# All 16,384 experts computed densely in place of gathered rows, in a two-block transformer kernel

## The chip, the core and the metric

The kernel runs on one core of a Trainium2 chip. A core has a matrix engine (TensorE, "PE" in the profile; its weight loads are "PEld"), a vector engine (VectorE, "DVE"), a scalar engine (ScalarE, "ACT"), GpSimd ("POOL", used here almost only to issue transfers), and SyncE ("SP", which issues the weight transfers). Sixteen DMA engines move data between DRAM and the on-chip memory SBUF; matrix products land in PSUM, eight banks of 128 x 512 floats. All data are 32-bit floats. The metric is the device time of one execution in microseconds (us), the median of three runs.

## The reference, cut to what matters

For 256 tokens of width 1024 a first block (attention with a chosen set of keys, a convolution branch, a mixture of experts called PEER, and a gated per-layer projection) is followed by a second block (a recurrent scan over a context and over the tokens, then a convolutional feed-forward). The change is in the experts and in the first part of the context's scan. Per token and for each of 8 heads, PEER forms two queries, scores each against 128 keys, takes the best 16 of either side, then the best 16 of the 256 pairs, which name 16 experts out of 128 x 128:

```python
def peer(h, w_query, sub_keys, expert_u, expert_v):
    q = (h @ w_query).reshape(B, S, PEER_HEADS, 2, PEER_HALF)
    sc = jnp.einsum('bshcd,hckd->bshck', q, sub_keys)
    sv, si = lax.top_k(sc, PEER_TOPK)
    ...
    cand_i = (si[..., 0, :, None] * N_KEYS + si[..., 1, None, :]).reshape(B, S, PEER_HEADS, n_cand)
    top_s, top_j = lax.top_k(cand_s, PEER_TOPK)
    eidx = jnp.take_along_axis(cand_i, top_j, axis=-1)
    gate = jax.nn.softmax(top_s.astype(jnp.float32), axis=-1).astype(h.dtype)
    ...
        u = expert_u[et]
        v = expert_v[et]
        act = jax.nn.gelu(jnp.einsum('tnd,td->tn', u, xt)) * gt
        return jnp.einsum('tn,tnd->td', act, v)
```

So 128 experts per token: a dot product with a row u of 1024, gelu, a gate, and a sum of rows v of 1024. Both tables hold 16,384 rows, 67.1 MB each.

## The kernel before, in words

One program per engine is written out by hand; engines meet only by semaphores. A list called order (from L2582) holds stages: all engines do a stage's functions one after the other. Dense products use two ring slots of weights (2 MB each, loaded by SP, L479 to L484: tile i waits until tile i-2 is used) and two halves of PSUM, G[0] and G[1]. The helper for a tile whose weights stand still (stationary) while 256 tokens stream is L502, the one with tokens stationary and 512 weight columns streaming is L512.

The stages are: projections and attention (L741 to L873), the mix (to 275 us of the trace), pe_queries (L1234 on: norm, first query tiles, first scores at L1260), then a stage called beside, then the gated projection (pe_ple, L741 and L752), the token scan (pe_x_in and the pairs), and the feed-forward (L502, L2454).

In the stage beside, POOL gathers for each of 256 steps (two blocks of 128 tokens, 128 selections each) one row of 8 KB for each of 128 partitions: u and v of one expert (L1475). Eight such row buffers are in flight. VectorE forms the dot product of a row's u half with the token (L1490), ScalarE applies gelu and the gate and builds a small diagonal (L1496, L1501, L1506), TensorE multiplies the diagonal with the v half and adds into PSUM (L1521), which frees the buffer. A list of pieces says what every engine does between two such groups: the other query tiles (L1269), the choice of experts by VectorE (dve_select, L1364 on), then the context: normed, transposed (L2147), projected (L2157), and the context's scan (L1741, L1751, L1808, L1822, L1942 and L1984 to L1988 in pe_pair, L2105). The context's weights and the last token block arrive by SP behind sp_ctx.

Of the kernel before, what the change touches and what calls it, by code (L numbers as in the profile page):

```python
# [19 lines left out]
F32 = mybir.dt.float32  # L20
# [36 lines left out]
RING = 8  # L57
GROUP = 2
QUADS, QP = 4, 32
# [21 lines left out]
def const_columns():  # L81


    widths = dict(ident=P, eps=1, gn_eps=1, flip=P, lower=CH, upper=CH, lower_eq=CH, upper_eq=CH, lower_neg=CH, upper_neg=CH, head_mean=P, head_mean2=2, conv_mean=P,
                  ident2=HD, hide=TB * T, reset=RC * T, iota=NCAND, ident_q=QP, quad=QUADS)
    at, out = 0, {}
    for name, n in widths.items():
        out[name] = (at, n)
        at += n
    return out, at  # L90


def consts_array():
# [27 lines left out]
    put("iota", np.arange(NCAND, dtype=np.float32)[None])  # L121
    put("ident_q", np.eye(QP)[i % QP])
    put("quad", (i[:, None] // QP) == np.arange(QUADS)[None])
# [18 lines left out]
def weight_tiles(dram):  # L142
# [28 lines left out]
    tile("ctx_k", part(w, 0, DC, K20, 512))  # L171
    tile("ctx_v", part(w, 0, DC, V20, 512))
    tile("ctx_lora", part(w, 0, DC, LORA0, 128), width=128)
    for i in range(2):
        tile(f"ple_proj{i}", part(dram["w_ple_proj"], 0, 2, 512 * i, 512))
# [16 lines left out]
def build(nc, dram, out_dram):  # L192
# [5 lines left out]
    with ExitStack() as ctx:  # L198
# [112 lines left out]
        r = Region()  # L311
        eidx = r.take(TB * NSEL, U32).rearrange("p (b n) -> p b n", b=TB)
        gate = r.take(TB * NSEL).rearrange("p (b n) -> p b n", b=TB)
        dots, gelu, acts = [r.take(RING).rearrange("p (g n) -> p g n", n=GROUP) for _ in range(3)]
        diag = r.take(RING * QP).rearrange("p (g n) -> p g n", g=RING)
        rows = r.take(RING * 2 * D).rearrange("p (g n) -> p g n", g=RING)
        high = r.take(2 * D).rearrange("p (g n) -> p g n", g=2)
        quad_ring = ring[:, tile_at["ple_proj0"] % WSLOTS, 1024:4096].rearrange("p (g n) -> p g n", g=QUADS - 1)
        after_rows = r.at

        carry = r.take(512)
        loraup = r.take(2 * 512).rearrange("p (d n) -> p d n", d=2)
        after_mod = r.at
        gatebc = Region(after_mod).take(2 * D).rearrange("p (g n) -> p g n", g=2)
        hold = after_mod + 2 * D

        qpT = chunks(16)
        qpT_end = r.at
        rest = r
        r = Region(ARENA - 3072)  # L330
        keysT = r.take(2 * PH * NK).rearrange("p (g n) -> p g n", g=2 * PH)
        gbc = r.take(D)
        r = rest
# [8 lines left out]
        tsc = r.take(HEADS * PK).rearrange("p (g n) -> p g n", g=HEADS)  # L342
# [3 lines left out]
        eif = r.take(HEADS * PK)  # L346
        gsum = r.take(HEADS)
        spread_e, spread_g = [r.take(HEADS * PK * QUADS) for _ in range(2)]
        assert r.at <= ARENA - 3072
        sel_end = r.at  # L350
# [3 lines left out]
        r = Region(after_mod)  # L354
        a2 = actT.rearrange("p c t -> p (c t)")
# [4 lines left out]
        def scan_memory(full, r, free, beside=None):  # L360
# [13 lines left out]
            m.b, m.kd = tile(), tile(free[0])  # L374
            m.cum, m.e = tile(), tile(free[1])
# [13 lines left out]
            if full:  # L389
# [5 lines left out]
        ctx_m = scan_memory(False, r, [a2[:, 0:1024], a2[:, 1024:2048]],  # L395
                            ring[:, tile_at["ctx_lora"] % WSLOTS, 1024:4096])
        ctx_end = r.at
# [8 lines left out]
        x_m = scan_memory(True, r, [r.take(1024), r.take(1024)])  # L406
# [13 lines left out]
        quad_last = Region(ctx_end).take(D)  # L420
        pT = normed[:, 0, 0:512].rearrange("p (k t) -> p k t", k=2)
        pproj = high
        sgate = Region(after_rows - 4096).take(2048).rearrange("p (b n) -> p b n", b=TB)
# [23 lines left out]

        ctok = Region(after_mod + 1024).take(TB * D).rearrange("p (b n) -> p b n", b=TB)
        cnormed = keysT.rearrange("p g n -> p (g n)").rearrange("p (b n) -> p b n", b=TB)
        assert ctx_m.lora.shape[-1] and after_mod + 3 * 1024 + T <= qpT_end  # L450
# [13 lines left out]

        def sp_weights(sp):
            for i, (name, width, parts) in enumerate(tiles):
# [4 lines left out]
                if name == "ctx_lora":  # L471
                    sp_ctx(sp)
                if name == "ple_proj1":
                    sp_last_tokens(sp)
                if name == "ple_gate0":
                    sp.wait_ge(S("cdone"), 1)
                    sp.wait_ge(S("dots_ok"), TB * GROUPS)
                if i >= WSLOTS:
                    sp.wait_ge(S("tile_done"), i - WSLOTS + 1)  # L479
                for view, kc, at, n in parts:  # L480
                    dst = ring[:, i % WSLOTS, 0:kc * width].rearrange("p (k n) -> p k n", n=width)
                    sp.dma_start(dst[:, :, at:at + n], view).then_inc(S(f"landed{i % WSLOTS}"), 16)
# [3 lines left out]
        def pe_tile(pe, name, buffer=True):  # L486
# [7 lines left out]
            return ring[:, i % WSLOTS, 0:kc * width].rearrange("p (k n) -> p k n", n=width), G[i % 2]  # L494
# [48 lines left out]
        ACT_LOADS = ("lora", "ctx", "pT", "gup", "fg")  # L543
# [9 lines left out]

        NORM_ORDER = ("nc",)

        def so_far(tag, per_norm, n):

            return NORM_ORDER.index(tag) * per_norm + n

        def act_norm(act, tag, src, dst, col, ready=(), gain=False):

            for b in range(1):
                for name, v in ready:
                    act.wait_ge(S(name), v)
                nc.scalar.activation(dst[:, b, :], src[:, b, :], ACT.Square,
                                     accum_out=stat[:, col + b:col + b + 1]).then_inc(S("norm_squares"), 1)
            act.wait_ge(S("norm_squares"), so_far(tag, TB, TB))
            nc.scalar.activation(stat[:, col + 2:col + 4], stat[:, col:col + 2], ACT.Sqrt, scale=1.0 / D,  # L570
                                 bias=K("eps")).then_inc(S("norm_root"), 1)
            if not gain:
                act.wait_ge(S("norm_recip"), so_far(tag, 1, 1))
                nc.scalar.activation(dst[:, 0, :], src[:, 0, :], ACT.Copy,
                                     scale=stat[:, col + 4:col + 5]).then_inc(S("normed_ok"), 1)

        def dve_norm(dve, steps, tag, src, dst, col, gain=None, ready=()):
            for name, v in ready:
                dve.wait_ge(S(name), v)
            nc.vector.tensor_tensor_reduce(dst[:, 1, :], src[:, 1, :], src[:, 1, :], 1.0, 0.0, ALU.mult, ALU.add,  # L580
                                           stat[:, col + 1:col + 2]).then_inc(S("norm_squares"), 1)
            dve.wait_ge(S("norm_root"), so_far(tag, 1, 1))
            nc.vector.reciprocal(stat[:, col + 4:col + 6], stat[:, col + 2:col + 4]).then_inc(S("norm_recip"), 1)
            dve.wait_ge(S("norm_recip"), so_far(tag, 1, 1))
            for b in range(TB) if gain is not None else (1,):
                r_ = stat[:, col + 4 + b:col + 5 + b]
                if gain is None:
                    ins = nc.vector.tensor_scalar(dst[:, b, :], src[:, b, :], r_, None, ALU.mult)
                else:
                    ins = nc.vector.scalar_tensor_tensor(dst[:, b, :], src[:, b, :], r_, gain, ALU.mult, ALU.mult)  # L590
                ins.then_inc(S("normed_ok"), 1)

# [2220 lines left out]
```

## Time and profile before

| | |
|---|---|
| three runs | 1559.96 us median (1553.43 to 1562.26) |
| span of the profiled execution | 1554.9 us, 5.1 us under the median |
| TensorE busy | 1212.9 us, 78% of the span |
| VectorE busy | 926.5 us, 60% |
| ScalarE busy | 431.5 us, 28% |
| moved by DMA | 409.73 MB, 264 GB/s mean |

The page gives for the profiled execution its span, from the first to the last instruction, and no other time of its own; the three times are those of runs without a profile. Two things about counts: a matrix product of 32-bit floats that is one line in the code stands as two MATMUL records, so a tile of 32 products shows x64; and the merged durations of the chain and the timeline are those to read, since single records overlap.

### The profile page before, as it was taken

Reading aid. Unit: us, or ns where it says so; the run is one execution under the profiler, and the core shown is the slowest. Engines: PE = TensorE matmul, PEld = TensorE weight load, DVE = VectorE, ACT = ScalarE, POOL = GpSimd, SP = SyncE. Lnnn points to the kernel's source line nnn. Section 1 sums busy time; section 2 is a strip of 40 time slices with the busy share of each in tenths; the row PEclk is TensorE's granted clock in tenths of the full one; section 3 lists DMA queues with packets and bytes.
Section 4 is the critical chain, followed back from the end, with each engine's and each line's share of the span. In section 5 each row is a group of like instructions: output and inputs, shape, how many; then the busy total and the mean of one; then the engine's idle time right before and its main releaser. Section 6 shows DMA issues by size and latency. Waiting matters only on the chain.

```text
span 1554.9 us, 26679 instructions
## 1 busy us (share of the span) xinstructions
PE 1212.9 (78%) x11282; PEld 834.9 (54%) x11282; DVE 926.5 (60%) x2067; ACT 431.5 (28%) x1094; POOL 347.1 (22%) x315
## 2 busy tenths in 40 slices
PE   7989898894385533457856775799987888999998
PEld 6467784772153100125524452468877774888843
DVE  2887666657797988785677655321455343455512
ACT  2111420132432422543364332423243211110100
POOL 1000012034354555454455544000000000000000
PEclk9997999996597855569878996899999999999999
DMA  9551459699999999999999999624300023344432
GB/s 381 195 191 66 144 205 390 238 383 419 414 410 420 420 422 421 421 414 419 416 421 420 420 418 418 240 82 163 109 9 3 4 111 108 122 163 161 137 140 104
DMA packets 109720, 409.73 MB, mean 264 GB/s; under 512 B 8456, under 2 KB 33552, under 8 KB 76448
## 3 DMA queue, kind: packets, MB, share of 16 engines
q0 software_dynamic: 44576, 297.35, 46.5%
q1 hardware_dynamic: 63552, 106.48, 19.2%
q10 hardware_dynamic: 1472, 4.20, 1.0%
q8 instruction: 88, 1.44, 0.4%
q14 instruction: 32, 0.26, 0.0%
HBM read 405.89 MB, written 2.11 MB: 262 GB/s over the span
## 4 chain that ended last, share of the span: by engine, by line
PE 58%; DMA 22%; DVE 10%; ACT 4%; issue 3%; POOL 2%; another core or an unknown queue 0%; POOLq 0%; DVEq 0%; ACTq 0%; SPq 0%
PE psum L502 20%; DMA arena<-in_experts,arena 17%; PE psum L1942 8%; PE psum L2454 5%; PE psum L512 4%; DVE arena L1490 4%; PE psum L1521 3%; DMA arena<-in_lora_up 2%; PE psum L755 2%; PE psum L1269 2%; POOL arena L1475 2%; PE psum L2244 2%; PE psum L760 2%; DMA arena<-in_ada_wT 2%; PE psum L741 2%
## 5 line engine op out<-in xcount | busy, mean ns | idle before, releaser
L1475 POOL DMA_INDIRECT arena<-in_experts,arena x256 | 317.1, 1239 | 383.2 <-PE psum L1521 299.8
L1521 PE MATMUL psum<-arena 128*32 128x512 f32 x1024 | 185.4, 805 | 238.2 <-ACT arena L1506 231.6
L502 PE MATMUL psum<-actT,weights 128*128 128x256 f32 x1312 | 287.3, 381 | 0.0
L502 PEld LDWEIGHTS psum<-actT,weights 128*128 128x128 f32 x1312 | 250.3, 191 | 35.7 <-issue 1.5
L1521 PEld LDWEIGHTS psum<-arena 128*32 128x32 f32 x1024 | 22.7, 121 | 329.5 <-ACT arena L1506 307.3
L1490 DVE CUSTOM_DVE_ANT_0 arena<-arena 128x1024 f32<-128x1024 f32 x96 | 116.7, 1224 | 50.9 <-DMA arena<-in_experts,arena 50.1
L1490 DVE CUSTOM_DVE_ANT_0 arena<-weights,arena 128x1024 f32<-128x1024 f32 x96 | 116.6, 1223 | 37.1 <-DMA arena<-in_experts,arena 35.1
L1496 ACT ACTIVATE arena<-arena 128x2 f32<-128x2 f32 x128 | 26.1, 204 | 364.3 <-DVE arena L1490 350.4
L1942 PE MATMUL psum<-arena 64*64 64x64 f32 (+1 forms) x2816 | 89.7, 231 | 17.4 <-DVE arena L2059 7.1
L1942 PEld LDWEIGHTS psum<-arena 64*64 64x64 f32 x2816 | 84.1, 142 | 26.0 <-issue 14.6
L1490 DVE CUSTOM_DVE_ANT_0 arena<-normed,arena 128x1024 f32<-128x1024 f32 x64 | 77.2, 1225 | 22.1 <-DMA arena<-in_experts,arena 20.3
L1119 POOL DMA_DIRECT2D arena<-in_ada_wT x48 | 25.5, 531 | 229.7 <-DVE mod L1135 229.7
L2454 PE MATMUL psum<-weights,arena 128*128 128x512 f32 x176 | 75.7, 592 | 0.0
L512 PE MATMUL psum<-weights,actT 128*128 128x512 f32 x160 | 69.2, 592 | 0.0
L1506 ACT ACTIVATE arena<-const,arena 128x32 f32<-128x32 f32 x256 | 66.3, 306 | 0.0
L1501 ACT ACTIVATE arena<-arena 128x1 f32<-128x1 f32 x256 | 61.5, 287 | 12.1 <-ACT arena L1496 0.4
L2528 DVE SCALAR_TENSOR_TENSOR arena<-arena,small 128x256 f32<-128x256 f32 x154 | 61.9, 478 | 0.0
L2454 PEld LDWEIGHTS psum<-weights,arena 128*128 128x128 f32 x176 | 33.4, 190 | 41.7 <-issue 41.6
L1942 PEld LDWEIGHTS psum<-actT,arena 64*64 64x64 f32 x1152 | 39.3, 134 | 21.4 <-ACT arena L2027 12.0
L512 PEld LDWEIGHTS psum<-weights,actT 128*128 128x128 f32 x160 | 30.4, 190 | 37.8 <-issue 37.8
L1942 PE MATMUL psum<-actT,arena 64*64 64x64 f32 x1152 | 45.5, 221 | 5.7 <-issue 4.3
L675 ACT ACTIVATE normed<-xres 128x512 f32<-128x512 f32 (+1 forms) x13 | 9.0, 692 | 146.4 <-DVE xres L2544 60.3
(390 smaller groups left out, 1897.0 us busy)
## 6 DMA issues: line engine op xcount, KB each, us to landing
weights<-in_w_in SPq DMA_DIRECT2D x18, 2048.0 KB
arena<-in_ada_wT POOLq DMA_DIRECT2D x48, 512.0 KB, 6.3
weights<-in_ffn_w_up SPq DMA_DIRECT2D x22, 1024.0 KB
weights<-in_ffn_w_down SPq DMA_DIRECT2D x5, 2048.0 KB
weights<-in_w_out SPq DMA_DIRECT2D x4, 2048.0 KB
weights<-in_w_peer_q SPq DMA_DIRECT2D x4, 2048.0 KB
arena<-in_experts,arena POOLq DMA_INDIRECT x256
weights<-in_w_ple_gate SPq DMA_DIRECT2D x2, 2048.0 KB
```

The costliest lines, as they stand in the source:

```text
L502: mm = nc.tensor.matmul(out[:, c * T:(c + 1) * T], w[:, k, c * P:(c + 1) * P], act[:, k, :], start=(k == 0), stop=(k == kc - 1))
L512: mm = nc.tensor.matmul(out[:, b * 512:(b + 1) * 512], act[:, k, b * P:(b + 1) * P], w[:, k, :], start=(k == 0), stop=(k == kc - 1))
L741: mm = nc.tensor.matmul(chunk_bank(c)[:, b * P:(b + 1) * P], xres[:, b, c * P:(c + 1) * P], norm_diag[:, b, :], start=True, stop=True)
L755: mm = nc.tensor.matmul(out[:, 2 * i * T:(2 * i + 1) * T], w[:, k, 2 * i * P:(2 * i + 1) * P], actT[:, k, :], start=(k == 0), stop=(k == D ...
L1475: nc.gpsimd.indirect_dma_start(out=rows[:, n % RING, :], out_offset=None, in_=dram["experts"], in_offset=bass.IndirectOffsetOnAxis(ap=eidx ...
L1490: ins = nc.vector.tensor_tensor_reduce(rows[:, pos, 0:D], quad_row(b, k % QUADS), rows[:, pos, 0:D], 1.0, 0.0, ALU.mult, ALU.add, dots[:, ...
L1501: nc.scalar.activation(acts[:, g, j:j + 1], gelu[:, g, j:j + 1], ACT.Copy, scale=gate[:, b, bass.ds(t * RING + (g * GROUP + j), 1)]).then_ ...
L1506: nc.scalar.activation(diag[:, pos, :], K("ident_q"), ACT.Copy, scale=acts[:, g, j:j + 1]).then_inc(S("diag_ok"), 1)
L1521: mm = nc.tensor.matmul(SUMS[sum_part(k, i), i, :], diag[:, pos, :], rows[:, pos, D + 512 * i:D + 512 * (i + 1)], start=first, stop=last, ...
L1942: mm = nc.tensor.matmul(dst[half[c], g, at + q * n:at + (q + 1) * n], left(g, c, q), right(g, c, q), start=True, stop=True)
L2454: return nc.tensor.matmul(aux[2 * b + n], ffT[:, f, b * P:(b + 1) * P], w[:, k, 512 * n:512 * (n + 1)], start=(f == 0), stop=(f == FC - 1))
L2528: st.run(nc.vector.scalar_tensor_tensor(dst, src, w, dst, ALU.mult, ALU.add))
```

## The change

The experts are no longer gathered. Their tables are laid out as 128 chunks of u and 128 chunks of v (one chunk: the 128 experts of one first key, 512 KB), and all are computed for all tokens:

- pe_keys_of, 128 times: 8 products with a 128 x 128 piece of the u chunk stationary and 256 tokens streaming. Two chunks fill a PSUM bank; ScalarE applies gelu into SBUF (act_gelu); POOL writes each pair's result to DRAM (dots_out), but for two pairs that are kept.
- The gates become a dense matrix gsel[expert i][expert j][token]: per token one product of two one-hot matrices (pe_onehots, dve_onehots, act_onehots), 256 in all.
- pe_values_of, after all keys: per pair of chunks VectorE multiplies the results, read back by POOL, with the gates (dve_values_of), and TensorE multiplies with the v chunks: per chunk 2 token blocks x 2 halves, 512 columns streaming, all added up in four PSUM banks.
- All four query tiles and the context's norm, transposes and three projections now come in pe_queries, ahead of the first key chunk. The context's scan and the choice of experts stand between the first 64 key chunks, the one-hot products between the other 64.
- The chunks use the ring of weights in eight parts (sp_experts). The projection of p (before two ring tiles) is made at the end in pe_ple from memory of its own. The normed rows in DRAM and their copies by quarters (quads) go.

```diff
-        def pool_rows(pool):
-            for n in range(TB * NSEL):
...
-                nc.gpsimd.indirect_dma_start(
-                    out=rows[:, n % RING, :], out_offset=None, in_=dram["experts"],
...
-                ins = nc.vector.tensor_tensor_reduce(rows[:, pos, 0:D], quad_row(b, k % QUADS), rows[:, pos, 0:D], 1.0, 0.0,
-                                                     ALU.mult, ALU.add, dots[:, g, j:j + 1])
...
-                    mm = nc.tensor.matmul(SUMS[sum_part(k, i), i, :], diag[:, pos, :], rows[:, pos, D + 512 * i:D + 512 * (i + 1)],
-                                          start=first, stop=last, skip_group_check=True)
...
+        def sp_experts(sp, first, last):
+            for s in range(first, last):
+                if s >= U_SLOTS:
+                    sp.wait_ge(S("exp_used"), s - U_SLOTS + 1)
...
+        def pe_keys_of(pe, c):
+            w = pe_chunk(pe, c).rearrange("p (k n) -> p k n", k=DC)
+            pair = c // 2
+            if c % 2 == 0 and pair >= 2:
+                pe.wait_ge(S("gelu_ok"), pair - 1)
+            at = (c % 2) * T
+            for k in range(DC):
+                mm = nc.tensor.matmul(dots_bank(pair)[:, at:at + T], w[:, k, :], actT[:, k, :],
+                                      start=(k == 0), stop=(k == DC - 1))
+            mm.then_inc(S("exp_used"), 1)
...
+        def pool_dots(pool):
+            for pair in range(PAIRS - KEPT):
+                pool.wait_ge(S("gelu_ok"), pair + 1)
+                pool.dma_start(dots_out[pair], dstage[:, pair % KEPT, :]).then_inc(S(f"dots_out{pair % KEPT}"), 16)
...
+            def sums(at, c, b, w):
+                lhs = weighted[:, at % ACT_SLOTS, c * T + b * P:c * T + (b + 1) * P]
+                for n in range(2):
+                    mm = nc.tensor.matmul(aux[2 * b + n], lhs, w[:, 512 * n:512 * (n + 1)], start=(at == 0 and c == 0),
+                                          stop=(at == PAIRS - 1 and c == 1), skip_group_check=True)
+                return mm
+            for at in range(PAIRS - LAST_PAIRS):
+                w = [pe_chunk(pe, NK + 2 * at + c) for c in range(2)]
+                for b in (1, 0):
+                    pe.wait_ge(S("weighted_ok"), TB * at + 2 - b)
...
+            for g in range(T // OH):
+                pe.wait_ge(S("onehot_ok"), g + 1)
...
+                for k in range(OH):
+                    mm = nc.tensor.matmul(PS[:, g % 4, k * P:(k + 1) * P], onehots[:, g % 2, 1, k, :],
+                                          onehots[:, g % 2, 0, k, :], start=True, stop=True)
...
         def pe_ple(pe):
+            pe.wait_ge(S("ple_in"), 32)
             pe.wait_ge(S("gatebc_ok"), 2)
+            for b in range(TB):
+                for n in range(2):
+                    for k in range(2):
+                        mm = nc.tensor.matmul(G[b][:, 512 * n:512 * (n + 1)], pT[:, k, b * P:(b + 1) * P],
+                                              pw[:, k, 512 * n:512 * (n + 1)], start=(k == 0), stop=(k == 1))
+                mm.then_inc(S("pproj_pe"), 1)
+            pe.wait_ge(S("pproj_ok"), TB)
             pe_norm_tile(pe, "n3", "ple_gate0", tokens=True)
...
+        SCAN_END = 64
+        turn = 0
+        for f in scan_stages(ctx_m, "c"):
+            spread(f, turn, turn + f["pieces"])
+            turn += f["pieces"]
...
+        spread(dict(pe=pe_onehots, act=act_onehots, dve=dve_onehots, pieces=T // OH + 3), SCAN_END, NK - 2)
```

TensorE before, in the stage beside, at the first expert groups (L1521) and the last query tiles (L1269; L1260 are scores):

```order
58 L1521 MATMUL psum<-arena 32x512 x4
59 L1260 MATMUL psum<-arena 128x128 x8
60 L1269 MATMUL psum<-actT,weights 128x256 x8
61 L1521 MATMUL psum<-arena 32x512 x4
62 L1269 MATMUL psum<-actT,weights 128x256 x8
63 L1521 MATMUL psum<-arena 32x512 x4
64 L1269 MATMUL psum<-actT,weights 128x256 x8
65 L1521 MATMUL psum<-arena 32x512 x4
```

TensorE now, where the key chunks begin (L1110 is pe_keys_of; L1250 context products, L1260 scores, L514 the three context projections, the rest pieces of the context's scan):

```order
57 L1260 MATMUL psum<-arena 128x128 x8
58 L1250 MATMUL psum<-arena 128x128 x8
59 L514 MATMUL psum<-normed,weights 128x256 x72
60 L1110 MATMUL psum<-actT,weights 128x256 x8
61 L1665 MATMUL psum<-const,arena 128x2 x8
62 L2119 MATMUL psum<-const,arena 128x128 x8
63 L1110 MATMUL psum<-actT,weights 128x256 x24
64 L1675 MATMUL psum<-const,stat 64x128 x16
65 L1110 MATMUL psum<-actT,weights 128x256 x8
66 L1734 MATMUL psum<-arena 128x256 x8
67 L1110 MATMUL psum<-actT,weights 128x256 x48
```

Between two pieces there stand now 8 products of 128 x 256 where there stood 4 of 32 x 512, and the projections stand ahead of all of it.

TensorE before in the context's solves (L1942), with expert groups between the levels:

```order
134 L1521 MATMUL psum<-arena 32x512 x4
135 L1942 MATMUL psum<-actT,arena 64x64 x16
136 L1942 MATMUL psum<-arena,actT 64x64 x16
137 L1942 MATMUL psum<-actT,arena 64x64 x16
138 L1521 MATMUL psum<-arena 32x512 x4
```

TensorE now in the same solves (L1868 is the former L1942), and further on the one-hot products (L1478):

```order
72 L1868 MATMUL psum<-arena 64x64 x48
73 L1110 MATMUL psum<-actT,weights 128x256 x8
74 L1868 MATMUL psum<-arena 64x64 x48
75 L1110 MATMUL psum<-actT,weights 128x256 x8
...
420 L1478 MATMUL psum<-normed 128x128 x4
421 L1110 MATMUL psum<-actT,weights 128x256 x8
422 L1478 MATMUL psum<-normed 128x128 x4
423 L1110 MATMUL psum<-actT,weights 128x256 x8
```

The solves keep their 48 products a level; what moved is that a whole key chunk follows each, and four one-hot products come between the later chunks.

SP's transfers now, from the first query tile to the gated projection:

```order
13 L493 DMA weights<-in_w_peer_q 128x8x512
14 L561 DMA arena<-in_ctx 128x2x1024
15 L493 DMA weights<-in_w_peer_q 128x8x512 x3
16 L561 DMA arena<-in_lora_up 128x2x512
17 L493 DMA weights<-in_w_in 128x8x512
18 L493 DMA weights<-in_w_in 128x8x128
19 L1093 DMA weights<-in_expert_u 128x1024 x3
20 L493 DMA weights<-in_w_in 128x8x512
21 L1093 DMA weights<-in_expert_u 128x1024 x125
22 L1093 DMA weights<-in_expert_v 128x1024 x128
23 L493 DMA weights<-in_w_ple_gate 128x8x512 x2
```

The context's tokens are loaded behind the first query tile now, and the expert chunks stand in SP's queue between the last context tile and the gated projection's weights.

## Rows read from the trace of the kernel before

**Rows 1.** The page: the slices, chain and dearest groups.
```profile
PEclk9997999996597855569878996899999999999999
DMA  9551459699999999999999999624300023344432
...
PE 58%; DMA 22%; DVE 10%; ACT 4%; issue 3%; POOL 2%; another core or an unknown queue 0%; POOLq 0%; DVEq 0%; ACTq 0%; SPq 0%
...
L1475 POOL DMA_INDIRECT arena<-in_experts,arena x256 | 317.1, 1239 | 383.2 <-PE psum L1521 299.8
L1521 PE MATMUL psum<-arena 128*32 128x512 f32 x1024 | 185.4, 805 | 238.2 <-ACT arena L1506 231.6
L502 PE MATMUL psum<-actT,weights 128*128 128x256 f32 x1312 | 287.3, 381 | 0.0
```
**Rows 2.** Stretches: us, busy (records) of PE, PEld, DVE, ACT, POOL; PEclk, DMA, GB/s.
```profile
297.40:995.20 697.80, 429.88 (x4761) 233.14 (x4761) 512.54 (x1284) 264.44 (x816) 317.15 (x256) 0.76 1.00 409
600.00:700.00 100.00, 47.22 (x396) 15.81 (x398) 81.13 (x166) 45.29 (x128) 50.27 (x40) 0.60 1.01 418
1334.00:1473.00 139.00, 139.00 (x645) 122.17 (x644) 76.36 (x190) 17.10 (x42) 0.00 (x0) 1.00 0.44 152
```
**Rows 3.** VectorE's busy time in L1490 alone, same first stretch.
```profile
297.40:995.20 697.80, 311.29 (x512) 0.76 1.00 409
```
**Rows 4.** Chain of waits, in order of time: start, us, what.
```profile
290.43 6.92 PE psum L760 x32
298.53 2.02 PE psum L1260 x16
300.56 13.83 PE psum L502 x64
...
995.20 2.90 PE psum L741 x12
...
1334.60 138.13 PE psum L502 x640
1472.73 75.55 PE psum L2454 x176
```
**Rows 5.** Timeline of TensorE at the first expert groups.
```profile
342.49 1.07 PE L1521 MATMUL psum<-arena 128*32 128x512 f32 x8
343.49 3.72 PE L1269 MATMUL psum<-actT,weights 128*128 128x256 f32 x16
347.14 1.06 PE L1521 MATMUL psum<-arena 128*32 128x512 f32 x8
```
**Rows 6.** The token scan's solves, L1942 and L1984 alone: us, PE, PEld, PEclk, DMA, GB/s.
```profile
1142.00:1272.00 130.00, 78.32 (x2528) 74.78 (x2528) 0.97 0.07 23
...
1142.00:1272.00 130.00, 11.55 (x128) 11.00 (x128) 0.97 0.07 23
```
**Rows 7.** Chain of waits in the token scan's start.
```profile
1057.54 1.68 PE psum L1741 x16
...
1073.14 1.90 PE psum L1751 x32
...
1082.96 1.93 PE psum L1808 x16
1084.89 7.10 PE psum L2244 x32
...
1119.62 1.75 PE psum L1822 x16
1121.37 3.46 PE psum L2244 x16
```
**Rows 8.** SP's transfers of two 1 MB tiles, and a product that waited for one.
```profile
217.33 7.27 SPq L482 DMA_DIRECT2D weights<-in_w_att_out  x2
...
231.46 3.72 PE L502 MATMUL psum<-arena,weights 128*128 128x256 f32 x16 [0.35 <-DMA weights<-in_w_att_out]
```
**Rows 9.** Timeline at the end of the gathers, all engines.
```profile
984.69 0.99 ACT L1625 COPY arena<-psum 128x1024 f32<-128x1024 f32 x1
...
989.76 1.94 PE L1521 MATMUL psum<-arena 128*32 128x512 f32 x8 [3.86 <-ACT arena L1506]
...
994.76 0.29 DVE L722 TENSOR_SCALAR normed<-const,stat 128x128 f32<-128x128 f32 x1
```
**Rows 10.** Groups of VectorE, 290 to 992: busy us, mean ns, idle before.
```profile
L2059 DVE TENSOR_TENSOR actT<-actT,psum 128x512 f32<-128x512 f32 x20 | 13.7, 687 | 30.8 <-PE psum L1942 30.8
```

More of the change, by code:

```diff
@@ L170, in weight_tiles @@
     w = dram["w_in_2"]
-    tile("ctx_k", part(w, 0, DC, K20, 512))
     tile("ctx_v", part(w, 0, DC, V20, 512))
     tile("ctx_lora", part(w, 0, DC, LORA0, 128), width=128)
-    for i in range(2):
-        tile(f"ple_proj{i}", part(dram["w_ple_proj"], 0, 2, 512 * i, 512))
+    tile("ctx_k", part(w, 0, DC, K20, 512))
     for i in range(2):
@@ L463, in build, with begin_of @@
             landed_at.append(16 * n_parts[i % WSLOTS])
+        def begin_of(name):
+            return 3072 if name == "ctx_lora" else 0
         def sp_weights(sp):
@@ L577, in dve_norm @@
[L577 to L591, printed above, removed]
@@ L1227, in act_quads, with ring_chunk @@
[L1227 to L1240 removed]
+        def ring_chunk(s):
+            return ring[:, (s % U_SLOTS) // 4, 1024 * (s % 4):1024 * (s % 4 + 1)]
@@ new lines, in act_values_of, with score_bank, ctx_bank @@
+        def act_values_of(act):
+            act_gelu(act, PAIRS - 1)
+            act.wait_ge(S("weighted_ok"), TB * (KEPT + PLE_CHUNKS // 2))
+            for g in range(2):
+                act.wait_ge(S("gatebc_pe"), g + 1)
+                nc.scalar.copy(gatebc[:, g, :], G[g]).then_inc(S("gatebc_ok"), 1)
+        def score_bank(b):
+            return aux[2 + b]
+        def ctx_bank(c):
+            free = G[tile_at["ctx_v"] % 2]
+            return (aux[0], aux[1], free[:, 0:512], free[:, 512:1024])[c % 4][:, 0:T]
@@ L1526, in groups_of_rows @@
-        def groups_of_rows(eng, group, b, first, last):
-            while first < last:
-                t, g = divmod(first, PER_TURN)
-                if g or t == 0 or last - first < 2 * PER_TURN:
-                    group(eng, b, t, g, GROUP)
-                    first += 1
-                else:
-                    end = min(last // PER_TURN, TURNS - 1)
-                    if group is act_group:
-                        eng.wait_ge(S("gates_done"), TB * QUARTERS)
-                    with eng.Fori(t, end) as i:
-                        for g in range(PER_TURN):
-                            group(eng, b, i, g, GROUP)
-                    first = PER_TURN * end
@@ L2655, in build, with spread @@
-        n_groups = TB * GROUPS
-        pieces[GROUPS + 4].append((len(beside), 0))
-        beside.append(dict(act=act_ple_load, pieces=1))
-        pieces[-1].append((len(beside), 0))
-        beside.append(dict(act=act_block0_squares, pieces=1))
-        assert len(pieces) < n_groups, len(pieces)
+        FIRST = 2
+        stage(dve=lambda dve, st: dve_select_first(dve, st, FIRST))
+        beside = []
+        pieces = [[] for _ in range(NK)]
+        def spread(f, begin, end):
+            n = f["pieces"]
+            for k in range(n):
+                pieces[begin + k * (end - begin) // n].append((len(beside), k))
+            beside.append(f)
```

825 lines of the change are left out of this document (327 added, 498 removed).

## The prediction

> **What bounds the kernel now.** I read the page first: its slices show the DMA share at 9 in a block from about a fifth of the span to three fifths, with TensorE's clock at 5 to 9 of ten there and at 9 almost everywhere else; the chain of waits gives TensorE 58% and DMA 22%; the dearest groups name the gathers, L1475 [rows 1]. Then the stretch from the end of the first query tile (290.43 + 6.92 = 297.35) to the first norm product of the gated projection (995.20) [rows 4]. In these 697.8 us the DMA share is 1.00 at 409 GB/s while TensorE is busy 429.9, VectorE 512.5 and ScalarE 264.4, none of them full, and the mean clock is 0.76; one hundred microseconds inside it show 418 GB/s, clock 0.60 and TensorE 47.2 busy [rows 2]. So the transfer bounds this stretch: 256 gathers of 128 rows of 8 KB are 268.4 MB, or 642 us at 418 GB/s, and TensorE's and VectorE's work lies beneath it. Ahead of it and behind it the chain is mostly TensorE: the feed-forward runs without a gap for 139.0 us at clock 1.00 with the DMA share at 0.44 [rows 2, 4].
>
> **What one product costs.** All rests on this. L502's 640 records from 1334.60 take 138.13 us [rows 4]. In the code these are ten tiles of 32 products, so a product is two records; the whole group has 1,312 records for 20.5 tiles [rows 1], which bears that out. One product of 128 x 256 is 138.13 / 320 = 0.432 us, one of 128 x 512 is 75.55 / 88 = 0.859 us (L2454, 176 records) [rows 4], weight loads and tile changes included, at full clock (2.4 GHz, PEclk 1.00).
>
> **The change, part by part.**
>
> Gone: 268.4 MB of gathers, 311.3 us of VectorE in L1490 [rows 3], L1521 and the small ScalarE steps. As the stretch is replaced as a whole, I count what stands there now. What transfers remain are 134.2 MB of chunks and 62 results of 256 KB written and read, 32.5 MB: 399 us at 418 GB/s, far beneath what follows.
>
> Front (first query tile to first key chunk). Three more query tiles at 13.83 [rows 4] are 41.5. Four sets of scores at 2.02, and 1.2 before the first (298.53 - 297.35) [rows 4], are 9.3. Sixteen context products of 128 x 128 at 1.75 / 8 = 0.22 [rows 7] are 3.5, with about 2 for ScalarE's copies between them. The three projections are 72 products at 0.432, 31.1. The last one's weights share a ring slot with the first, so SP issues them only when that is used, with the short one (3.5) as cover. A 1 MB tile issued when a slot came free near 224.3 was waited for until 231.46 [rows 8], 7.2 us; 2 MB are at least 5.0 at 418 GB/s and at most twice 7.2, and I take 7.5, nearer the low end because no other load runs beside it: 4.0 of wait (1.5 to 11). The context's 1 MB comes earlier now, beside the modulation weights: 2.5 later for all. Sum 93.9; before, part of this lay under the transfer.
>
> Key phase. 1,024 products of 128 x 256 are 442.0. The context's scan: L1942 has 2,432 records there, at 78.32 / 2528 = 0.031 each [rows 6] 75.3; the second half of four pairs 11.6 (L1984, with its two neighbours in between) [rows 6]; two directions of four steps at 1.75 to 1.93, 15.4; the common part 1.68 + 1.90 + 1.75 [rows 7], 5.3; the chain of states, 64 products, 4: together 111.6. Before, these lay under the gathers. Between 64-wide and 128-wide products a change costs something: 8 products of L1269 beside L1521 take 3.65 (343.49 to 347.14) [rows 5] where 3.45 is the sum, and 16 of L2244 after L1808 take 7.10 where 6.91 is the sum [rows 7]. I take 0.3 for going and coming, 45 times: 13.5. The 256 one-hot products cost 0.22 each, 56.1, and 0.1 for each of 64 groups, since 16 records of L1822 and then L2244 show no more than the sum [rows 7]: 62.4. Transposes of experts and gates: 3.
>
> Waits in the key phase are the unknown cost, since no row of before shows these engines together. At least nothing: a chunk of 3.45 follows each piece, VectorE needs 0.69 for a level's sum [rows 10], and its load is half: 512.5 - 311.3 = 201 us is all else that it does in the old stretch [rows 2, 3], to which one-hots add 64 x (4 x 0.29 [rows 9] + 0.69 [rows 10]) = 118, against 1,000 us. At most about 1 us in each of the 63 turns with a piece of the scan, if the choosing of experts, which stands behind each piece on VectorE, makes the next piece wait: 63. I take 10, near the low end, as the chunk is five times the step that it hides. Sum of the key phase: 442.0 + 111.6 + 13.5 + 62.4 + 3 + 10 = 642.5.
>
> Value phase. 512 products of 128 x 512 at 0.859: 439.8. Sixteen products of 128 x 128 for the modulation's gates, 3.5; 1 at the seam, since two pairs are kept in SBUF and the next results have 13.7 us to arrive. VectorE's two products per pair are small beside 6.9 us of TensorE. Sum 444.3. If the read-back did not keep up, TensorE would wait for it; but four slots are 27 us ahead.
>
> Tail. The projection of p moved behind the last chunk: 8 products, 6.9, then a copy by ScalarE, 0.99 [rows 9], and a hop: 8.2 from the last value product to the norm's first, in place of 995.20 - (989.76 + 1.94) = 3.5 [rows 4, 9]. The norm's square sums and roots run beside it. From there on the program is the same, and its 560 us are taken over.
>
> Sum: 93.9 + 642.5 + 444.3 + 8.2 = 1,188.9 in place of 697.8, which is 491 more. The profiled execution would go from 1554.9 to 2046; the median lies 5.1 us above its span, so the forecast is **2051 us**, a ratio of 1.31.
>
> One rule would change the sum. The row says 0.859 for a 32-bit product of 512 columns [rows 4]. The Trainium skill (TensorE: Matmul & The Clock Gate, Back-to-back issue gap) gives a sustained spacing of about 131 ns per matmul at 512 columns, and N / 2.4 + 2.5 ns for a lone one; another page of the Trainium skill (FP8 and Floating Point Precision, TensorE Precision Notes) says that true 32-bit floats take four passes. By 131 ns the value phase would be an estimated 268 us, by the other formula 442. The trace agrees with the second, and a rival below carries the first.
>
> **Rivals.**
>
> Transfer still bounds. The change halves the bytes; if TensorE fitted beneath them, the stage would last 399 us, and 1560 - 697.8 + 93.9 + 399 + 8.2 = 1363: faster. For it: the DMA share of 1.00 and 409 GB/s [rows 2]. It decides from the point where a chunk's 8 products cost less than its landing, 512 KB at 418 GB/s = 1.25 us, or 0.157 a product. Against it: 0.432 in a gapless row, 2.8 times as much.
>
> A record is a product. Were 0.216 and 0.429 the full prices, both phases would lose half, 441: 1610, slower still. Against it: the count of tiles in the code.
>
> Short passes in the value phase: products of 512 columns at 0.524, so 512 x 0.335 = 171 less: 1880. Against it: 176 records at 0.429, and nothing in the value phase differs from them in shape. This is the page's first figure.
>
> The key phase waits at every turn of the scan, the high end above: 53 more, 2104. For it: VectorE and ScalarE are in line, and a solve's level waits for both. Against it: the chunk between.
>
> **How the numbers follow.** The forecast, with its small terms off by up to 40 in all (the front's wait, the changes of width, waits of 0 to 40): 0.77, 2010 to 2090. Waits at every turn: 0.16, 2090 to 2150. Short passes: 0.02; a record is a product: 0.01; transfer bounds: 0.01; still cheaper small terms, 1980 to 2010: 0.03. The range that leaves out under two in ten is 2010 to 2115. A measurement of this kernel tells 0.5% (8 us) from no change. Faster by more: 0.01; within it: 0.01, for a mixture of the cases that I have not seen; slower: 0.98.
>
> **What would show it.** In the new profile the group of L1110 should have 2,048 records and 442 us, the values' products (1,024 records) 440, both without a gap longer than a wait; PEclk 9 from the front to the end; DMA share 0.3 to 0.5 there, some 170 MB in place of 268; VectorE and ScalarE under half. The first key chunk should begin near 391, the first value product near 1034, the norm near 1486. The prediction is wrong if a product of L1110 takes clearly less than 0.43, if the clock sinks in the long run of products, or if TensorE sits idle for more than 40 us in the key phase, and then the releaser tells whether it was VectorE's choice, ScalarE's gelu or a chunk.

## The result: 2022.7 us, 1.297 times the time before

The changed kernel takes 2022.71 us (median of 4 runs, 2019.42 to 2023.77), the kernel before 1559.78 (4 runs); the ratio is 1.2971, with a 95% interval of 1.2940 to 1.3003. The forecast was 2051 in a range of 2010 to 2115. The profiled execution has a span of 2021.5 us, 24.5 below the 2046 that the sum gave for it. The section behind the experiments goes through these 24.5 us, and through the other 4 by which the median missed.

The page of the changed kernel, its slices and its chain (answering to [rows 1]):

```profile
PE   8989889899999999999999999999999978899998
...
DVE  3966655163373334444211111111123353435531
...
PEclk9979989999999999999999999999999999999999
DMA  9334874343343344444466555555324100244542
...
PE 93%; DMA 2%; DVE 2%; ACT 1%; issue 1%; DVEq 0%; POOL 0%; POOLq 0%
```

The block of 9s in the DMA row is gone and a block of 9s in the PE row has taken its place; where TensorE pauses no more, the granted clock stays at 1.00, the upper of its two levels. DMA's 22% of the chain became 2%.

The stages in windows (answering to [rows 2]; columns as there). They are the front, the key phase up to the last piece of the scan, the key phase with the one-hot products, the value phase, and all that follows:

```profile
302.42:394.46 92.04, 85.68 (x433) 76.02 (x434) 29.69 (x148) 15.28 (x24) 0.00 (x0) 0.98 0.36 126
394.46:735.90 341.44, 341.20 (x4148) 297.10 (x4148) 162.92 (x557) 94.26 (x143) 17.31 (x32) 1.00 0.39 132
735.90:1006.47 270.57, 270.57 (x1499) 244.96 (x1498) 106.72 (x312) 53.09 (x95) 16.23 (x30) 1.00 0.44 150
1006.47:1449.51 443.04, 443.04 (x1058) 198.13 (x1057) 49.10 (x127) 5.25 (x7) 35.49 (x65) 1.00 0.57 189
1449.51:2021.50 571.99, 528.61 (x5449) 409.94 (x5447) 217.65 (x409) 114.04 (x207) 0.00 (x0) 0.98 0.29 100
```

In 1,055 us of keys and values TensorE is idle for 0.24 us, while the DMA engines are half idle. Two groups of rows say where that time lies: TensorE's groups in the key phase, and the products of the value phase.

```profile
L1110 PE MATMUL psum<-actT,weights 128*128 128x256 f32 x2048 | 464.6, 381 | 0.0
L1868 PE MATMUL psum<-arena 64*64 64x64 f32 (+1 forms) x2432 | 75.5, 222 | 0.0
L1478 PE MATMUL psum<-normed 128*128 128x128 f32 x512 | 66.8, 275 | 0.0
L1910 PE MATMUL psum<-arena 64*64 64x64 f32 x128 | 11.6, 243 | 0.0
...
L1665 PE MATMUL psum<-const,arena 128*128 128x2 f32 x16 | 1.9, 250 | 0.2 <-DVE arena L1697 0.2
```

```profile
L1178 PE MATMUL psum<-weights,normed 128*128 128x512 f32 x1024 | 439.8, 592 | 0.0
```

A warning on reading the first: 464.6 us for the keys is more than they cost. A matmul's end is modelled, and the last record of each of 128 chunks overhangs the next piece by 0.17 us. The price is the distance between starts. In the timeline of TensorE (start, us, line), where a turn is one key chunk and the piece that stands beside it, a chunk of 8 products takes 3.45 us (from 850.72 to 854.17) and the 4 one-hot products of a turn 0.90:

```profile
849.83 1.05 PE L1478 MATMUL psum<-normed 128*128 128x128 f32 x8
850.72 3.62 PE L1110 MATMUL psum<-actT,weights 128*128 128x256 f32 x16
854.17 1.05 PE L1478 MATMUL psum<-normed 128*128 128x128 f32 x8
855.07 3.62 PE L1110 MATMUL psum<-actT,weights 128*128 128x256 f32 x16
```

128 x 3.45 is 442, as [rows 4] had said.

### The profile page after: what moved, and what is told of

It reads as the page before. It is cut to its first block, busy times and chain, and to the rows that moved or that the text cites. A ratio compares the mean times of both kernels' runs of the same rounds, so it can differ in the third digit from the quotient of the medians.

```text
span 2021.5 us, 31021 instructions
## 1 busy us (share of the span) xinstructions
PE 1935.2 (96%) x13670; PEld 1423.5 (70%) x13670; DVE 763.0 (38%) x1935; ACT 340.7 (17%) x559; POOL 98.2 (5%) x185
## 4 chain that ended last, share of the span: by engine, by line
PE 93%; DMA 2%; DVE 2%; ACT 1%; issue 1%; DVEq 0%; POOL 0%; POOLq 0%
PE psum L1110 22%; PE psum L1178 22%; PE psum L514 18%; PE psum L1868 8%; PE psum L2320 4%; PE psum L524 3%; PE psum L1478 3%; PE psum L688 1%; DMA arena<-in_ada_wT 1%; PE psum L2110 1%; PE psum L693 1%; PE psum L674 1%; PE psum L1910 1%; PE psum L685 1%; PE psum L806 1%
## 5 line engine op out<-in xcount | busy, mean ns | idle before, releaser
L1110 PE MATMUL psum<-actT,weights 128*128 128x256 f32 x2048 | 464.6, 381 | 0.0
L1178 PE MATMUL psum<-weights,normed 128*128 128x512 f32 x1024 | 439.8, 592 | 0.0
L1110 PEld LDWEIGHTS psum<-actT,weights 128*128 128x128 f32 x2048 | 380.5, 190 | 51.2 <-issue 1.5
L1178 PEld LDWEIGHTS psum<-weights,normed 128*128 128x128 f32 x1024 | 194.5, 190 | 244.0 <-issue 243.9
L514 PE MATMUL psum<-actT,weights 128*128 128x256 f32 x1440 | 315.5, 381 | 0.0
L514 PEld LDWEIGHTS psum<-actT,weights 128*128 128x128 f32 x1440 | 274.8, 191 | 39.1 <-issue 1.5
L1160 DVE TENSOR_TENSOR normed<-actT,arena 128x256 f32<-128x256 f32 x124 | 47.1, 421 | 367.9 <-PE psum L1178 363.9
L1868 PE MATMUL psum<-arena 64*64 64x64 f32 (+1 forms) x4864 | 151.5, 223 | 16.8 <-DVE arena L1985 7.1
L1868 PEld LDWEIGHTS psum<-arena 64*64 64x64 f32 x4864 | 143.3, 136 | 30.6 <-issue 21.7
L1499 DVE TENSOR_SCALAR normed<-const,arena 128x128 f32<-128x128 f32 x256 | 71.5, 343 | 150.0 <-PE psum L1478 150.0
L1478 PEld LDWEIGHTS psum<-normed 128*128 128x128 f32 x512 | 66.6, 192 | 3.1
L1478 PE MATMUL psum<-normed 128*128 128x128 f32 x512 | 66.8, 275 | 0.0
```

The source lines that it names most:

```text
L514: mm = nc.tensor.matmul(out[:, c * T:(c + 1) * T], w[:, k, c * P:(c + 1) * P], act[:, k, :], start=(k == 0), stop=(k == kc - 1))
L1110: mm = nc.tensor.matmul(dots_bank(pair)[:, at:at + T], w[:, k, :], actT[:, k, :], start=(k == 0), stop=(k == DC - 1))
L1160: nc.vector.tensor_tensor(by_token(weighted[:, at % ACT_SLOTS, :])[:, :, tb], by_token(src)[:, :, tb], gsel[b][:, 2 * pair:2 * pair + 2, : ...
L1178: mm = nc.tensor.matmul(aux[2 * b + n], lhs, w[:, 512 * n:512 * (n + 1)], start=(at == 0 and c == 0), stop=(at == PAIRS - 1 and c == 1), s ...
L1478: mm = nc.tensor.matmul(PS[:, g % 4, k * P:(k + 1) * P], onehots[:, g % 2, 1, k, :], onehots[:, g % 2, 0, k, :], start=True, stop=True)
L1499: nc.vector.tensor_scalar(onehots[:, g % 2, 0, k, :], K("iota"), sel_i[:, at:at + 1], sel_g[:, at:at + 1], ALU.is_equal, ALU.mult)
```

## Experiments

The theory to be tested: TensorE's price of a 32-bit product bounds both phases, the transfer of the tables lies beneath with room to spare; before, the transfer bounded. The main rival: the transfer or its latency still holds the products up. Experiments 1, 4, 6 and 7 leave out part of the data or of the products and so measure time alone; 2, 3 and 5 compute the same function with the experts' products rounded to 16 bits (bfloat16). Experiments 1, 2, 4, 6 and 7 were timed once each, and four runs of the changed kernel spread over 4.4 us, so the readings rest on the windows.

**1. Half of every chunk (e3).** The loads are cut, the products are as many and as large:

```diff
-                sp.dma_start(ring_chunk(s), src).then_inc(S(f"exp_in{s % U_SLOTS}"), 16)
+                sp.dma_start(ring_chunk(s)[:, 0:512], src[:, 0:512]).then_inc(S(f"exp_in{s % U_SLOTS}"), 16)
...
-                mm = nc.tensor.matmul(dots_bank(pair)[:, at:at + T], w[:, k, :], actT[:, k, :],
+                mm = nc.tensor.matmul(dots_bank(pair)[:, at:at + T], w[:, k % 4, :], actT[:, k, :],
...
-                    mm = nc.tensor.matmul(aux[2 * b + n], lhs, w[:, 512 * n:512 * (n + 1)], start=(at == 0 and c == 0),
+                    mm = nc.tensor.matmul(aux[2 * b + n], lhs, w[:, 0:512], start=(at == 0 and c == 0),
```

> The changed kernel with half of every expert chunk loaded (512 of its 1,024 columns, 67 MB less in all); the products are as many and as large, and use the loaded half twice. Theory: the key phase stays at 612 us and the value phase at 443 us, total 2,023 +- 6; the DMA share falls from 0.39 to about 0.2 and from 0.57 to about 0.3. Rival (transfers hold the products up, the products' own price is less than it looks): each phase shortens, down to half, total 1,500 to 1,950.

Measured: 2018.09 us in one run. Its windows of the key phase and the value phase:

```profile
392.43:1004.40 611.97, 611.73 (x5645) 542.01 (x5645) 269.72 (x869) 147.32 (x238) 33.54 (x62) 1.00 0.25 84
1004.40:1447.30 442.90, 442.90 (x1057) 198.01 (x1056) 49.13 (x127) 5.26 (x7) 35.49 (x65) 1.00 0.38 118
```

Both phases last as long as with all the bytes (611.97 against 612.01, 442.90 against 443.04) at 84 and 118 GB/s. The transfer costs the changed kernel nothing; the rival falls. The 4.6 us in the total lie outside these windows, 2.0 of them before the first chunk, and are no more than the spread of the runs.

**2. Cheaper products, values alone (e1).** A chunk is rewritten as bfloat16 in its own place by ScalarE, the weighted results are written so by VectorE, and the products read both:

```diff
+        def short(a):
+            return a.bitcast(BF16)[:, 0:a.shape[-1]]
+
+        def act_short(act, s):
+            act.wait_ge(S(f"exp_in{s % U_SLOTS}"), 16 * (s // U_SLOTS + 1))
+            nc.scalar.copy(short(ring_chunk(s)), ring_chunk(s)).then_inc(S("short_ok"), 1)
...
-                    mm = nc.tensor.matmul(aux[2 * b + n], lhs, w[:, 512 * n:512 * (n + 1)], start=(at == 0 and c == 0),
+                    mm = nc.tensor.matmul(aux[2 * b + n], lhs, short(w)[:, 512 * n:512 * (n + 1)], start=(at == 0 and c == 0),
```

> The changed kernel with 16-bit operands in the value products alone: ScalarE rewrites each value chunk as bfloat16 in its own place (128 copies of 128x1024, the trace's pass of that shape took 1.05 us), VectorE writes the weighted activations as bfloat16; the key phase is untouched. Theory (TensorE's price of 32-bit products, 0.859 us each of 128x512, bounds the value phase): the price falls to about a quarter, 0.215 us, so the phase falls from 443.0 to 222 us (1,024 products, 220, and 2 of seams), total 2022.7 - 221 = 1,802 us (1,785 to 1,850). Rival 1 (a transfer bounds the phase): it stays at 443, total 2,023. Rival 2 (the rewriting on ScalarE or VectorE's weighting, 135 and 54 us, joins in with its latency): 250 to 300, total 1,830 to 1,880.

Measured: 1791.84 us in one run, 231 less. The time lies near the forecast, but the forecast's working was wrong: I counted records as products. There are 512 products, so a quarter of 439.8 is 110 us and not 220. The window of the value phase shows what else filled it:

```profile
1005.75:1217.25 211.50, 133.09 (x534) 52.31 (x544) 48.14 (x125) 134.01 (x131) 33.86 (x62) 0.94 1.01 393
```

TensorE is busy for 133 of 211.5 us, and the DMA share is 1.01 at 393 GB/s. The price of a product fell as the theory says, and the transfer, hidden until then, became the bound. So the rival is right from a certain price on, which experiments 4 and 5 look at.

**3. Cheaper products in both phases (e2).** The normed tokens and the key chunks are rewritten too, two chunks ahead of TensorE:

```diff
-            w = pe_chunk(pe, c).rearrange("p (k n) -> p k n", k=DC)
+            w = short(pe_chunk(pe, c)).rearrange("p (k n) -> p k n", k=DC)
...
+            pe.wait_ge(S("short_ok"), c + 2)
...
+            for s in range(0 if c == 0 else c + 2, min(c + 3, NK)):
+                act_short(act, s)
```

> As the run before, and the key products with 16-bit operands too (ScalarE rewrites the normed tokens once and each key chunk, two chunks ahead). Theory: the value phase is 222 us; the key phase's own TensorE work is 442/4 = 110 of keys and 170 of scan, selection and one-hot products, 280 us; but now each scan turn is a chain of TensorE, ScalarE and VectorE that the key products used to cover, and a one-hot turn is bounded by VectorE (4 x 0.343 + 0.685 = 2.06 us) and ScalarE (1.06 + 0.59 + 0.30 = 1.95 us), so 64 turns of 2.2 and 64 of 2.7 to 4.5 make 315 to 430 us; I take 330. Total 302 + 92 + 330 + 222 + 8 + 564 + 2 = 1,520 us (1,470 to 1,620), which would be faster than the kernel before (1,560). Rival (what the time hangs on is moving 166 MB): phases near their transfers, 200 and 190 us, total 1,360. Rival (only the stages' order matters, not the price of a product): no change from 1,800.

Measured: 1522.31 us (4 runs, 1521.34 to 1525.08), 0.9776 of the kernel before (0.9751 to 0.9802). The interval lies below 1, so all experts computed densely now beat the gathers, though by little more than 2%. Windows of the key phase in two halves (scan, then one-hots) and of the value phase, and the profile's waits of TensorE and of ScalarE in the last of them (us in total, times, longest):

```profile
390.92:582.00 191.08, 151.01 (x2862) 127.33 (x2864) 135.96 (x459) 133.62 (x179) 13.57 (x25) 0.87 0.59 187
582.00:741.70 159.70, 148.22 (x1764) 136.73 (x1762) 133.30 (x412) 135.24 (x193) 21.85 (x40) 0.99 0.89 318
741.71:952.96 211.25, 132.82 (x534) 52.33 (x544) 48.33 (x125) 134.58 (x132) 33.98 (x62) 0.94 1.00 392
```

```profile
PE psum L1194 <- ACT weights L1105: 71.7, 43, 6.4
PE psum L1194 <- DVE normed L1176: 9.5, 10, 1.2
```

```profile
ACT weights L1105 <- DMA weights<-in_expert_v: 72.3, 113, 2.4
```

Read together, in the value phase TensorE names ScalarE as what it waits for, and ScalarE waits for the chunk's landing. The key phase is 351 us, inside the 315 to 430 that were foretold, but the 64 turns with the scan took 3.0 us each and not 2.2, and the other 64 took 2.5, under the foretold 2.7 to 4.5. TensorE is idle there for some 52 us, where the changed kernel has 0.2; its two largest waits there are for ScalarE, for gelu and for a rewritten chunk:

```profile
PE psum L1119 <- ACT arena L1127: 14.4, 4, 4.2
PE psum L1119 <- ACT weights L1105: 12.1, 6, 3.9
```

The total came out at the 1,520 forecast with errors that cancelled (key phase 21 us more; value phase 11 less, and for another reason than the one given; 8 less around them). The price of a 16-bit product is again a distance between starts. Eight key products take 0.88 us in this run's chain of waits:

```profile
702.73 0.87 PE psum L1119 x8
703.61 0.89 PE psum L1500 x8
```

That is 0.110 each against 0.432, a factor of 3.9. At the end of the value phase in experiment 5 (below), 16 products without a wait between them take 3.45 us, from 924.03 to the next group's start at 927.48, at a granted clock of 1.00:

```profile
924.03 3.61 PE L1194 MATMUL psum<-weights,normed 128*128 128x512 bf16 x16 [2.96 <-issue]
927.48 7.03 PE L1595 MATMUL psum<-arena 128*128 128x512 f32 x16
```

That is 0.216 each against 0.859, a factor of 4.0. The Trainium skill (FP8 and Floating Point Precision, TensorE Precision Notes) says that true 32-bit floats take four passes; the trace agrees, with 3.9 and 4.0.

**4. Half of every chunk, with cheap products (e7).** Experiments 1 and 3 in one, with ScalarE rewriting the loaded half alone:

```diff
-                sp.dma_start(ring_chunk(s), src).then_inc(S(f"exp_in{s % U_SLOTS}"), 16)
+                sp.dma_start(ring_chunk(s)[:, 0:512], src[:, 0:512]).then_inc(S(f"exp_in{s % U_SLOTS}"), 16)
...
-            nc.scalar.copy(short(ring_chunk(s)), ring_chunk(s)).then_inc(S("short_ok"), 1)
+            nc.scalar.copy(short(ring_chunk(s))[:, 0:512], ring_chunk(s)[:, 0:512]).then_inc(S("short_ok"), 1)
```

> The kernel with 16-bit products in both phases, with half of every expert chunk loaded and rewritten (512 of 1,024 columns, used twice); the products are as many and as large. Theory (the transfer bounds the value phase at 392 GB/s, with 133 us of TensorE work beneath): 33.5 MB less brings the transfer to 126 us, so TensorE takes over: 140 us in place of 211; the second half of the key phase falls from 160 to its TensorE work, 150; total 1,522 - 71 - 10 = 1,441 us (1,425 to 1,470). Rival (TensorE's price of 16-bit products is not yet a quarter, it bounds at 211): 1,510 to 1,522.

Measured: 1452.33 us in one run. The second half of the key phase and the value phase:

```profile
582.00:736.00 154.00, 147.51 (x1701) 135.71 (x1698) 133.29 (x412) 104.56 (x191) 22.85 (x40) 0.99 0.61 193
736.00:885.54 149.54, 123.26 (x545) 51.94 (x546) 48.23 (x125) 79.80 (x131) 34.10 (x63) 0.98 0.95 339
```

The value phase fell from 211 to 150 us; the same cut that did nothing to the changed kernel is worth 62 us here. It stopped 10 us above the forecast: the DMA share is still 0.95, and TensorE still waits for 27 us, most of it for ScalarE and so for chunks:

```profile
PE psum L1194 <- ACT weights L1105: 17.9, 12, 3.9
PE psum L1194 <- DVE normed L1176: 9.2, 12, 1.0
```

ScalarE's rewriting was halved as well, so this run alone does not tell it from the transfer; experiment 5 leaves ScalarE's work as it is.

**5. The key results in 16 bits too (e5).** With four staged in place of two, so that they wait in half the bytes:

```diff
-KEPT = 2
+KEPT = 4
...
-        dstage = r.take(KEPT * 512).rearrange("p (s n) -> p s n", s=KEPT)
+        dstage = r.take(KEPT * 256).bitcast(BF16).rearrange("p (s n) -> p s n", s=KEPT)
...
-        dots_out = nc.dram_tensor("dots_out", (PAIRS - KEPT, P, 2 * T), F32, kind="Internal").ap()
+        dots_out = nc.dram_tensor("dots_out", (PAIRS - KEPT, P, 2 * T), BF16, kind="Internal").ap()
```

> The kernel with 16-bit products in both phases, with the key results kept, written to DRAM and read back as bfloat16 too (62 x 256 KB each way become 60 x 128 KB) and four of them staged in place of two. In the run with 16-bit products the value phase stood at a DMA share of 1.00 and 392 GB/s for 211 us, and the second half of the key phase at 0.89 and 318 GB/s. Theory (with the products cheap, the transfer bounds the value phase): 8.2 MB less to read is 8.2 / 0.392 = 21 us less there, 190 us; the second half of the key phase loses some of its waits for the stage's slots, 0 to 15 us; total 1,522 - 21 - 8 = 1,493 us (1,480 to 1,503). Rival (the value phase is held by the latency of eight slots and by ScalarE's rewriting, not by bytes): 1,512 to 1,522.

Measured: 1496.88 us (5 runs, 1495.65 to 1502.35), 0.9612 of the kernel before (0.9593 to 0.9632), the fastest version here that leaves nothing out. The second half of its key phase and its value phase:

```profile
582.00:735.30 153.30, 145.92 (x1663) 134.19 (x1662) 133.97 (x414) 131.82 (x189) 21.11 (x39) 0.99 0.84 286
735.30:927.64 192.34, 126.54 (x545) 50.55 (x546) 46.88 (x121) 134.22 (x131) 32.26 (x59) 0.98 1.01 392
```

The rate is the same 392 GB/s and the time fell by 18.9 us where 8.2 MB at that rate are 21: bytes, not slots or ScalarE (134 us as before), bound it. The second half of the key phase is 6.4 us shorter; with the 18.9 that is nearly all of the 25.4. These versions round the experts' products to 16 bits, which the kernel before does not.

**6. A quarter of the one-hot products (e6).**

```diff
-                for k in range(OH):
+                for k in range(1):
                     mm = nc.tensor.matmul(PS[:, g % 4, k * P:(k + 1) * P], onehots[:, g % 2, 1, k, :],
```

> The changed kernel with 64 of its 256 one-hot products (one of each group of four); all passes that make the one-hots and that evict the gates stay. Theory (TensorE's work in the key phase adds up without gaps, and a one-hot product costs 0.22 us with nothing for its group): 192 x 0.22 = 42.5 us less, all of it in the second half of the key phase, a turn falls from 4.34 to 3.68 us; total 2,023 - 42.5 = 1,980 us. Rival (the prediction's own term: 0.1 us for each group beside 0.22 for each product): the turn stays 0.1 us above that, 3.78 us, total 1,987. Rival (VectorE's 2.06 us or ScalarE's 0.9 us of a turn bound it): no change.

Measured: 1978.18 us in one run; the turn is 3.68 us in its timeline (two records of one product, then the chunk's 16):

```profile
850.26 0.39 PE L1478 MATMUL psum<-normed 128*128 128x128 f32 x2
850.48 3.62 PE L1110 MATMUL psum<-actT,weights 128*128 128x256 f32 x16
853.94 0.38 PE L1478 MATMUL psum<-normed 128*128 128x128 f32 x2
854.16 3.62 PE L1110 MATMUL psum<-actT,weights 128*128 128x256 f32 x16
```

One product costs 0.22 us, the group nothing. The window 733.00 to 960.60 is 227.60 us in place of 270.57: 43.0 less, where 42.5 were foretold. In this phase TensorE's work simply adds up.

**7. The kernel before with half rows (e4).** It uses the u half in place of v as well:

```diff
-                    out=rows[:, n % RING, :], out_offset=None, in_=dram["experts"],
+                    out=rows[:, n % RING, 0:D], out_offset=None, in_=dram["experts"],
...
-                    mm = nc.tensor.matmul(SUMS[sum_part(k, i), i, :], diag[:, pos, :], rows[:, pos, D + 512 * i:D + 512 * (i + 1)],
+                    mm = nc.tensor.matmul(SUMS[sum_part(k, i), i, :], diag[:, pos, :], rows[:, pos, 512 * i:512 * (i + 1)],
```

> The kernel before with gathered rows of half the size (only the 1,024 columns of u, which are used in place of v as well): 134 MB less, as many gathers, passes and products. Theory (the transfer at 409 GB/s bounded the 698 us stretch): it shortens until the next engine holds it, VectorE with 512.5 us of work, or TensorE with 430, with the latency of the ring of 8 rows on top: 540 us (515 to 600), total 1,560 - 158 = 1,402 (1,377 to 1,462). Rival (the stretch was a chain of waits from a row's landing to its release, the transfer ran beneath): 660 to 698, total 1,520 to 1,560.

Measured: 1459.80 us in one run. The stretch is 600.3 us long in place of 697.8. Its window, and VectorE's longest waits in it:

```profile
298.26:898.57 600.31, 403.74 (x4760) 217.71 (x4760) 505.15 (x1282) 263.38 (x816) 315.62 (x256) 0.79 0.77 254
```

```profile
DVE actT L2059 <- PE psum L1942: 25.9, 16, 3.5
DVE arena L1490 <- DMA arena<-in_experts,arena: 10.9, 10, 1.9
```

In the kernel before, the same view has VectorE waiting for gathers (L1490) for 105.4 us:

```profile
DVE arena L1490 <- DMA arena<-in_experts,arena: 105.4, 104, 2.0
```

So the transfer did bound the stretch, and 94.5 us less of waiting for it are nearly all of the 97.5 us that went. Half the bytes gave back only that: VectorE is now busy for 505 of 600 us, and its longest wait is for the context's scan, 25.9. I had expected 158 and sized VectorE's other waits too low; 600 is the edge of the forecast.

## Why the prediction was right, and which terms were off

The mechanism and the bound were right: the unit prices of [rows 4], 0.432 and 0.859 us, carried over to new lines unchanged (442 and 439.8 us), with TensorE at clock 1.00 in both places. What was off, in the order of the prediction's parts, adds up to the 24.5 us; nearly all of it is small terms of the key phase that were set too high, and nothing large cancelled:

- **The context's load, 2.5 us foretold, 5.1 seen** up to the end of the first query tile (302.42 against 297.35). Much of this is scatter: up to there the kernels of experiments 1 and 2 are the same as the changed one, and in them the first query tile ends 2.0 and 3.8 us earlier. In the profiles of all seven dense kernels the first query tile ends 1.3 to 5.1 us later than in the kernel before, 2.7 on the mean.
- **The front, 91.4 foretold without that load, 92.0 seen.** The wait for the last weights was sized at 4.0; the chain of waits has their transfer from 370.85 until the product at 378.71, and TensorE idle for 4.4 of it:

```profile
364.99 5.84 PE psum L514 x27
370.85 7.82 DMA weights<-in_w_in
378.71 15.75 PE psum L514 x64
```

- **The key phase, 642.5 foretold, 612.0 seen: the whole miss.** The keys were right. Waits of TensorE, taken as 10, are 0.2: a chunk of 3.45 us hid every step of the scan and of the choice, as the low bound had it. The 0.1 for each group of one-hots does not exist (57 us in place of 62.4; experiment 6). The scan's groups are 106.5 in place of 111.6, since the two directions are 9.9 (L1734 and L1748, 80 records) and not 15.4: I had priced all of their four steps like one of 8 products. Transposes are 0.6 in place of 3. What is left for the changes of width is 612.0 - 442.0 - 57.0 - 106.5 - 0.6 - 0.2 = 5.7 in place of 13.5. A solve's turn shows one such change: from 460.81 to 467.40 are 6.59 us, of which the 8 products take 3.65 in place of 3.45, so 0.2 and not 0.3, with 2.94 for the solve between. At 0.2 the 45 changes would be 9; the scan's groups are taken by their busy times, which hold an overhang of 0.08 for each solve (3.02 against 2.94), and that is about the difference:

```profile
457.86 3.02 PE L1868 MATMUL psum<-arena 64*64 64x64 f32 x96
460.81 3.72 PE L1110 MATMUL psum<-actT,weights 128*128 128x256 f32 x16
464.46 3.02 PE L1868 MATMUL psum<-arena 64*64 64x64 f32 x96
467.40 3.72 PE L1110 MATMUL psum<-actT,weights 128*128 128x256 f32 x16
```

- **The value phase, 444.3 foretold, 443.0 seen; the tail, 8.2 and 8.0.** No wait for the read-back showed.
- **The rest, taken over at 559.7, is 564.0.** The program is the same; 3.0 of the 4.3 us lie in the token scan, where short pauses in which TensorE waits for nothing that the profile shows differ by some tenths of a microsecond each. In the six other dense kernels the same stretch is 556.9 to 564.7 us. No run tells the 4.3 apart from scatter, and it stays open.
- **From span to median, 5.1 foretold, 1.2 seen** (2022.71 against 2021.5). This is the rest of the miss of 28.3 us in the median. A run's time lies 1.8 to 2.1 us above its own span wherever both are known here; the rest of the 5.1 was that the profiled execution of the kernel before was a quicker one than its median.

Of the foretold marks these held: no gap, 2,048 and 1,024 records, 442 us of keys by the distance between starts and 440 of values, clock, and 169.6 MB between the first chunk and the last. These did not: the DMA share was foretold at 0.3 to 0.5 and is 0.57 in the value phase; the first value product began at 1006.3 and not near 1034, and the norm at 1457.5 and not near 1486, which is the key phase's miss less the front's lag. Of the rivals, waits at every turn and short passes are refuted by the rows, a record as a product by the count, and a transfer that still bounds by experiment 1.

## What to carry to other kernels

Before trading gathered bytes for dense products, price both. Here a chunk of 512 KB lands in 1.3 us at the 404 GB/s of the value phase's middle in experiment 3; its eight 32-bit key products take 3.45 us, eight 16-bit ones 0.88. The type of the operands decided the outcome here: the same dense plan was 30% slower than the gathers in 32 bits and 4% faster in 16, and only then did halving the bytes matter. When long gapless products stand between the steps of a dependent chain, the chain can cost its TensorE work alone, as here (0.2 us of waits); waits are to be looked for when the products become short, as in experiment 3 (some 52 us idle in the key phase).

## What the runs showed that I had not expected

- A 32-bit product is two MATMUL records, a 16-bit one a single record: 1,024 records of 0.859 / 2 us became 512 at 0.216. The prices differ by the factor 4.0 only if both are counted in products.
- In the first half of the key phase the granted clock was 1.00 with 32-bit products (TensorE busy 341.2 of 341.4 us) and 0.87 with 16-bit ones (busy 151 of 191). In the value phase of experiment 3 it was 0.94, with pauses of up to 6.4 us.
- Rewriting a chunk of 128 x 1024 from 32 to 16 bits on ScalarE, in its own place, took 1.05 us, less than the 1.3 us that the chunk's 512 KB take at 404 GB/s; that it did not set the pace of the value phase is what experiment 5 shows.
